# Boxes of a blocked triangular inverse requested ahead of weight tiles, with joins, sums and scaling at other places, in a hybrid decoder layer on one core

## Chip, core and metric

The kernel runs on one core of one Trainium2 chip. The metric is the device time of one execution in microseconds (us). The profile covers one execution; its span starts with the first instruction that the profile shows.

## What is computed

One decoder layer on 256 tokens of width 1024, in float32:

```python
proj = einsum('bsd,de->bse', rms_norm(h), w_in)
q, k, v = silu(causal_conv(proj[gdn part]))          # 8 heads of 128
a_mat = strict_lower(beta * k k^T * decay) + eye     # per head and chunk
u, w = triangular_solve(a_mat, [v * beta, k * beta * exp(g)])
o_a = gated delta rule with u, w over the chunks
y_a = (rms_norm(o_a) * silu(z)) @ w_branch_gdn
y_f = softmax(q_f k_f^T / 8 + forget terms) v_f @ w_branch_fox   # 16 heads of 64
h = h + (sigmoid(g_a) * y_a + sigmoid(g_f) * y_f) @ w_out
h = h + moe(rms_norm(h))       # 64 experts, top 8, plus a shared one
h = h + sigmoid(rms_norm(h) @ w_pg) * rms_norm(p @ w_ple)
```

The kernel takes chunks of 128 tokens, so there are 16 triangular problems of 128 x 128 (8 heads, 2 chunks).

## The kernel before

**Stages.** The convolved projections (12 products), then pairs of projection tiles, attention, the branch projections, and at the end the 32 pairs of experts, whose weights (6 MB a pair) stream through a ring of three slots.

**Pairs of tiles.** The weights of the projections come as tiles of 1024 x 512 (2 MB), numbered 0 to 23, into a ring of three buffers (`load(t)`, line 482). From tile 6 on two tiles make a pair: f0 (6, 7), f2 (8, 9), f4 (10, 11), z (12, 13), m0, m2, ya, yf, wo. A pair is multiplied in Strassen's manner: seven half products of four matmuls' worth of chunks (8 recorded matmuls, line 1084) instead of eight. They are numbered 1, 5, 2, 6, 3, 7, 4 (`product`, line 1087), need sums of token blocks, four sums of weight blocks (`weight_sum(p, k)`, lines 1861 to 1884) and are put together by `join(p, k)` (lines 1886 to 1906) on VectorE, with copies kept by ScalarE (`keep`, line 826). Parts 1 and 2 fill bank A, 5 and 3 bank C, 6 and 7 bank B, 4 bank D. Part 7 waits until join 6 of its pair is made (`u_made`). For f0, f2 and f4 the sums 1 and 3 are made by DMA: SyncE requests the first half block (`begin_sum`), GpSimd adds the second onto it (`add_first`, `add_third`). From z on VectorE makes them: `weight_sum(z, 1)` adds the left upper blocks of both tiles of the pair (line 1867) and so waits for tiles 12 and 13; part 5 of z waits for it.

**Banks.** The eight PSUM banks are handed out by a list written before the kernel (`bank_fills`, `placed`): each fill names its set of banks and takes the next of that set in turn. A fill waits until the fill before in its bank is drained. The half products of f0, f2 and f4 share FOX_BANKS = (7, 1, 2); the small products beside them (kk, bb, qk) take SIDE_BANKS = (4, 5, 6, 0, 3). By that list f4.A takes the bank of f2.C, which join 3 of f2 drains.

**The inverse.** The 16 problems are cut into diagonal blocks of 32 x 32, 64 in all. When VectorE has finished the blocks (bb.0 to bb.3, line 1930), SyncE writes the diagonal blocks to DRAM in four requests (`box_blocks`, line 506) and reads them back as 64 rows of 1024 words (line 508). VectorE inverts all 64 by a substitution of 31 steps of two operations (lines 1947 and 1949), behind some of which stand joins of f2 (JOINED) and sums of f4 (SUMMED). A copy (line 1954) makes the transposed inverse. `unbox_inverses` writes both to DRAM (line 513, two requests of 256 KB) and reads them back into the full matrices (line 518, eight requests of 64 KB). P5, X5, V5, P6 and V6 (lines 1247 and 1254) then build the inverse of 128 x 128 between the half products of z.

**Order of SyncE.** Its list is fixed, and a request that waits holds all behind it. Around the change it reads: tile 9, tile 10, box_blocks, a wait for qk.3, begin_sum(f4), tile 11, tile 12, tile 13, unbox_inverses, tile 14. Tile 11 waits for part 6 of f2, tile 12 for part 7 of f2, tile 13 for part 6 of f4 and the sum 4 of f4, tile 14 for part 7 of f4.

**Order of VectorE** behind the substitution: joins 6, 3, 7, 4 of f4, sums 1 and 3 of z, the scaling (two small and two large products, lines 1981 to 1988), fox_squares(0, 0) and (0, 1) (lines 1969 and 1970: squares of half a token block and their sums), the copy of cT, sum 2 of z, fox_squares(1, 0), sum 4 of z, fox_squares(1, 1).

Of the kernel before, what the change touches and what calls it, by code (L numbers as in the profile page):

```python
# [54 lines left out]
FOX_BANKS, SIDE_BANKS = (7, 1, 2), (4, 5, 6, 0, 3)  # L55
# [4 lines left out]
PAIRED = ("f0", "f2", "f4", "z", "m0", "m2", "ya", "yf", "wo")  # L60
F0_, F2_, F4_, Z_, M0_, M2_, YA_, YF_, WO_ = range(9)
# [6 lines left out]
OPENS = {1: "A", 5: "C", 6: "B", 4: "D"}  # L68
# [5 lines left out]
def bank_fills():  # L74

    f = ["ncols", "xT.0.0", "xT.0.1", "xT.1.0", "xT.1.1"]
    f += ["qkv.0", "cols", "smallT", "qkv.1", "small", "qkv.2", "cum", "qkv.3", "gbT"]
    for c in range(4, 8):
        f += [f"qkv.{c}", f"gb.{c - 4}", TQ_BESIDE[c]]
    for c in range(8, 12):  # L80
        f += [f"qkv.{c}", TQ_BESIDE[c]]
    f += ["tq.0.4", "tq.1.4"]
    g = [(name, ALL_BANKS) for name in f]
    for p, k, beside in FOX_ORDER:
        if k in OPENS:
            g += [(f"{PAIRED[p]}.{OPENS[k]}", FOX_BANKS)]
        g += [(b, SIDE_BANKS) for b in beside]
    g += [(name, ALL_BANKS) for name in ("cT", "z.A", "P5", "z.C", "X5", "V5", "P6.0", "P6.1", "z.B")]
    g += [("V6.0", (0,)), ("V6.1", (1,))]
    f = ["z.D"]  # L90
    for j in range(2):
        f += [f"tg.{j}", f"wT.{j}", f"u0.{j}"]
    for j in range(2):
        f += [f"o0.{j}", f"s1.{j}"]
    for j in range(2):
        f += [f"u1.{j}"]
    for j in range(2):
        f += [f"o1.{j}"]
    f += ["m0.A", "cb.0", "m0.C", "cb.1", "cb.2", "m0.B", "cb.3", "cb.4", "m0.D"]
    g += [(name, ALL_BANKS) for name in f]  # L100

    g += [(f"fT.0.{j}", HEAD_BANKS) for j in range(4)] + [("m2.A", PAIR_BANKS)]
    g += [(f"fT.1.{j}", HEAD_BANKS) for j in range(4)] + [(f"oT.{n}.{j}", HEAD_BANKS) for n in range(NT) for j in range(2)]
    g += [(name, HEAD_BANKS) for name in ("cb.5", "cb.6", "cb.7")] + [("m2.C", PAIR_BANKS)]
    g += [(f"s.{i}", HEAD_BANKS) for i in range(4)]
    for i in range(8):
        for p, k in BESIDE_ATTENTION[i]:
            if k in OPENS:
                g += [(f"{PAIRED[p]}.{OPENS[k]}", PAIR_BANKS)]
        g += [(f"pT.{2 * i}", HEAD_BANKS), (f"pT.{2 * i + 1}", HEAD_BANKS)]  # L110
        if i < 6:
            g += [(f"s.{2 * i + 4}", HEAD_BANKS), (f"s.{2 * i + 5}", HEAD_BANKS)]
        g += [(f"pv.{i}", HEAD_BANKS)]
    g += [(f"yf.{q}", PAIR_BANKS) for q in "ACBD"]
    g += [(f"pT2.{n}", HEAD_BANKS) for n in range(NT)]
    g += [(f"mT.{n}.{j}", HEAD_BANKS) for n, j in BLOCKS] + [("e.0.0", HEAD_BANKS)]
    g += [(f"wo.{q}", PAIR_BANKS) for q in "ACBD"]
    f = [f"hT.0.{j}" for j in range(2)] + ["e.0.1", "e.1.0"] + [f"hT.1.{j}" for j in range(2)]
    g += [(name, LAST_BANKS) for name in f]
    return g + [("e.1.1", (1,)), ("routerT", (0,)), ("router", (2,)), ("sg", (7,)), ("rank", (4,))]  # L120
# [14 lines left out]
def program(nc, x, p, norm_mix, w_in, conv_w, a_log, dt_bias, gdn_norm, fox_f_bias, q_norm, k_norm,  # L135
# [3 lines left out]
    with ctx:  # L139
# [227 lines left out]
        def ps(name):  # L367
            return bank[place[name][0]]

        def wait_filled(eng, name):  # L370
            b, turn = place[name]
            eng.wait_ge(filled[b], turn + 1)
# [14 lines left out]
        W_QKV, W_PAIRED = 0, 6  # L387
# [74 lines left out]
        def _(sp):  # L462
# [62 lines left out]
            for t in range(3, len(wtiles) - 1):  # L525
                if t == W_PAIRED:
                    begin_sum(F0_)
                if t == W_PAIRED + 3:
                    sp.wait_ge(qkss, 8)
                    begin_sum(F2_)  # L530
                if t == W_PAIRED + 5:
                    box_blocks()
                    wait_filled(sp, "qk.3")
                    begin_sum(F4_)
                if t == W_PAIRED + 2 * Z_ + 2:
                    unbox_inverses()
                load(t)

# [1164 lines left out]
        def _(dve):  # L1703
# [48 lines left out]
            for c2 in range(12):  # L1752
                nm = f"qkv.{c2}"
                wait_filled(dve, nm)
                for s in range(4):
                    for i in range(2):
# [4 lines left out]
                        if s == 0:  # L1761
                            k = step(v.tensor_scalar(dst, src, wcol, None, ALU.mult))
                        else:
# [4 lines left out]
                            else:  # L1768
                                k = step(ins)
# [90 lines left out]
            def weight_sum(p, k):  # L1860

                b00, b01, b10, b11 = halves_of(p)
                if k == 1:
                    for i in range(2):
                        tile = W_PAIRED + 2 * p + i
                        dve.wait_ge(w_loaded[tile % A_SLOTS], 16 * (tile // A_SLOTS + 1))
                    ins = v.tensor_tensor(wdif[p], b01, b00, ALU.add)
                if k == 3:
                    dve.wait_ge(t_made, sums_made(p, 1))
                    ins = v.tensor_tensor(b01, b11, b01, ALU.add)  # L1870
                if k == 2:
                    if p < Z_:
                        tile = W_PAIRED + 2 * p + 1
                        dve.wait_ge(w_loaded[tile % A_SLOTS], 16 * (tile // A_SLOTS + 1))
                        dve.wait_ge(sum1_made, 16 * (p + 1))
                    else:
                        dve.wait_ge(t_made, sums_made(p, 1))
                    dve.wait_ge(half_filled, 3 * p + 1)
                    ins = v.tensor_tensor(b00, b11, wdif[p], ALU.add)
                if k == 4:  # L1880
                    dve.wait_ge(t_made, sums_made(p, 2))
                    dve.wait_ge(half_filled, 3 * p + 2)
                    ins = v.tensor_tensor(wdif[p], b10, b00, ALU.add)
                ins.then_inc(t_made, 1)

            def join(p, k):

                name = PAIRED[p]
                d01, d11, d10 = (result(p, n, j) for n, j in BLOCKS[1:])
                if k == 6:  # L1890
                    dve.wait_ge(kept, 2 * p + 1)
                    dve.wait_ge(half_filled, 3 * p + 3)
                    v.tensor_tensor(d01, ps(f"{name}.B")[:, :], m1[p], ALU.subtract).then_inc(u_made, 1)  # L1893
                if k == 3:
                    wait_filled(dve, f"{name}.C")
                    dve.wait_ge(u_made, p + 1)
                    close(v.tensor_tensor(d01, d01, ps(f"{name}.C")[:, :], ALU.add), f"{name}.C")  # L1897
                if k == 7:
                    wait_filled(dve, f"{name}.B")
                    close(v.tensor_tensor(d10, m1[p], ps(f"{name}.B")[:, :], ALU.subtract), f"{name}.B")  # L1900
                    dve.wait_ge(kept, 2 * p + 2)
                    wait_drained(dve, f"{name}.B")
                    v.tensor_tensor(d11, m5[p], d10, ALU.subtract).then_inc(c11_made, 1)
                if k == 4:
                    wait_filled(dve, f"{name}.D")
                    close(v.tensor_tensor(d10, d10, ps(f"{name}.D")[:, :], ALU.add), f"{name}.D")
# [33 lines left out]
            dve.wait_ge(l_loaded, 16)  # L1940
            dve.wait_ge(zeroed, 1)
            lb, xb = (q.rearrange("p (i j) -> p i j", i=BLK) for q in (lblk, xblk))
            JOINED, SUMMED = {11: 6, 17: 3, 20: 7, 21: 4}, {22: 2, 25: 4}
            for k in range(BLK - 1):
                m = BLK - 1 - k
                outer = rank1[:, 0:m * (k + 1)].rearrange("p (i j) -> p i j", i=m)
# [7 lines left out]
            v.tensor_copy(vblk.rearrange("p (j i) -> p j i", j=BLK), xblk.rearrange("p (i j) -> p j i", i=BLK)).then_inc(solved, 1)  # L1954

            join(F4_, 6)
            join(F4_, 3)
            join(F4_, 7)
            join(F4_, 4)
            for p in (F0_, F2_):  # L1960
                for q in "ACBD":
                    wait_drained(dve, f"{PAIRED[p]}.{q}")
# [2 lines left out]
            def fox_squares(n, half):  # L1965

                src = fox[:, n, D * half:D * half + D]

                seq(v.tensor_tensor(at(TPB, 1024), src, src, ALU.mult))
                ins = v.tensor_reduce(f_ss[:, n, 16 * half:16 * half + 16], at(TPB, 1024).rearrange("p (a b) -> p a b", a=16), AX.X, ALU.add)  # L1970
                if half:
                    ins.then_inc(fss, 1)
                    dve.wait_ge(fss, n + 1)
                else:
                    seq(ins)

            weight_sum(Z_, 1)
            weight_sum(Z_, 3)
            dve.wait_ge(geg, 2)
            dve.wait_ge(tq_copied, 6)  # L1980
            seq(v.tensor_tensor(be_s, eg_s, gb[:, 16:32], ALU.mult))
# [4 lines left out]
            k1 = qk[:, 1, D:2 * D].rearrange("p (h d) -> p h d", h=GH)  # L1986
            v.tensor_tensor(q1, q1, bc(eg_s[:, 8:16], 2, P), ALU.mult).then_inc(scaled, 1)
            v.tensor_tensor(k0, k0, bc(et_s[:, 0:8], 2, P), ALU.mult).then_inc(scaled, 1)

            fox_squares(0, 0)  # L1990
            fox_squares(0, 1)
            wait_filled(dve, "cT")
            close(v.tensor_copy(rowsT[:, 1, :], ps("cT")[0:48, 0:P].bitcast(BF16)), "cT")
            weight_sum(Z_, 2)
# [92 lines left out]
            for g in range(8):  # L2087
                if g < 7:
                    maxima(g + 1)
                f = 2 * g  # L2090
# [98 lines left out]
            k = [step(onto(n, j, m1[WO_], ALU.subtract if j else ALU.add)) for n, j in BLOCKS[1:]]  # L2189
# [282 lines left out]
```

## Time and profile before

| | |
|---|---|
| median of 3 runs | 902.4 us (901.75 to 904.97) |
| the profiled execution | 902.0 us |
| its span | 900.3 us |
| TensorE busy (PE) | 882.2 us, 98% |
| VectorE busy (DVE) | 521.0 us, 58% |
| ScalarE busy (ACT) | 196.3 us, 22% |
| GpSimd busy (POOL) | 58.2 us, 6% |
| moved by DMA | 275.53 MB, mean 306 GB/s |
| first small products of f0's pair to the last of z's | 103 to 224 us of the span |
| expert stage | 414 to 867 us of the span |

Busy time is the time in which an engine runs an instruction. SP is SyncE, PEld TensorE's weight loads. A row of a timeline gives start, duration, engine, line, operation, output from inputs, shape, count, and in brackets the idle time of the engine before it and what ended that.

### The profile page before, as it was taken

The page shows a single profiled execution, that of the slowest core. Times are in us where ns is not written, and L with a number is a line of the kernel's source. Part 1 is how long each engine was busy: PE and PEld are TensorE (multiplying, and loading weights), DVE is VectorE, ACT ScalarE, POOL GpSimd, SP SyncE. Part 2 cuts the span into 40 slices and gives each one's busy share as a digit, 9 for nine tenths or more (in the row PEclk, how much of TensorE's full clock was granted, in tenths as well). Part 3 has the DMA queues.
Part 4 walks back from the last instruction along what each step waited for, and adds up shares of the span by engine and source line. Part 5 has one row for each costly group of instructions (what it writes and reads, how often), then busy time and mean ns, then how long its engine had stood idle before and what let it go on. Part 6 is the DMA issues. An engine that isn't in the chain of part 4 may idle for free.

```text
span 900.3 us, 21078 instructions
## 1 busy us (share of the span) xinstructions
PE 882.2 (98%) x9169; PEld 503.8 (56%) x9170; DVE 521.0 (58%) x975; ACT 196.3 (22%) x398; POOL 58.2 (6%) x78
## 2 busy tenths in 40 slices
PE   7999999899999999999999999999999999999997
PEld 6888754345745454456555555555555555555543
DVE  3656866967677886865434345343435444445367
ACT  2214200012426651242111111101011111111122
POOL 2011200106200000020000000000000000000010
PEclk9999999999999999999999999999999999999999
DMA  8653888774151438978999999999999999999951
GB/s 247 228 202 110 225 275 247 194 234 148 40 186 47 141 117 333 383 307 332 401 421 420 423 421 422 422 422 422 422 422 422 422 422 422 422 422 422 415 209 49
DMA packets 69188, 275.53 MB, mean 306 GB/s; under 512 B 11498, under 2 KB 14171, under 8 KB 44315
## 3 DMA queue, kind: packets, MB, share of 16 engines
q1 hardware_dynamic: 67114, 268.68, 75.6%
q0 software_dynamic: 2016, 6.29, 3.7%
q8 instruction: 27, 0.44, 0.2%
q14 instruction: 15, 0.11, 0.0%
q10 hardware_dynamic: 16, 0.00, 0.0%
HBM read 269.99 MB, written 1.84 MB: 302 GB/s over the span
## 4 chain that ended last, share of the span: by engine, by line
PE 87%; DVE 6%; DMA 3%; ACT 1%; SPq 1%; issue 1%; POOL 0%; DVEq 0%; POOLq 0%; ACTq 0%
PE bank L1554 25%; PE bank L1084 17%; PE bank L1535 13%; PE bank L1199 9%; PE bank L1505 5%; PE bank L1518 5%; PE bank L1663 2%; PE bank L1061 2%; PE bank L1574 1%; DMA lbox<-arena 1%; PE bank L1153 1%; DVE arena L1949 1%; DVE arena L1947 1%; PE bank L1463 1%; PE bank L1474 1%
## 5 line engine op out<-in xcount | busy, mean ns | idle before, releaser
L1554 PE MATMUL bank<-arena 128*32 128x256 f32 x4096 | 227.2, 379 | 0.3 <-DVE arena L2278 0.3
L1554 PEld LDWEIGHTS bank<-arena 128*32 128x32 f32 x4096 | 132.8, 110 | 100.5 <-issue 18.6
L1084 PE MATMUL bank<-arena 128*128 128x512 f32 x344 | 154.4, 597 | 1.6 <-DVE arena L1893 1.6
L1535 PE MATMUL bank<-arena 128*32 128x512 f32 x1024 | 116.5, 595 | 0.5 <-ACT arena L991 0.5
L1084 PEld LDWEIGHTS bank<-arena 128*128 128x128 f32 x344 | 63.6, 190 | 77.1 <-issue 76.6
L1199 PE MATMUL bank<-actT,arena 128*128 128x256 f32 x384 | 85.3, 380 | 0.4 <-DVE actT L1731 0.4
L1199 PEld LDWEIGHTS bank<-actT,arena 128*128 128x128 f32 x384 | 72.0, 190 | 10.4 <-issue 1.1
L989 ACT ACTIVATE arena<-bank 128x256 f32<-128x256 f32 x32 | 12.3, 384 | 267.9 <-PE bank L1554 267.9
L2329 DVE COPY arena<-bank 128x512 f32<-128x512 f32 x32 | 22.1, 692 | 81.9 <-PE bank L1535 81.9
L2314 DVE SCALAR_TENSOR_TENSOR arena<-arena,gslot,bank 128x256 f32<-128x256 f32 x32 | 15.4, 480 | 90.0 <-ACT arena L989 90.0
L1084 PE MATMUL bank<-arena,actT 128*128 128x512 f32 x144 | 65.2, 596 | 2.3 <-DVE arena L1897 2.3
L1535 PEld LDWEIGHTS bank<-arena 128*32 128x32 f32 x1024 | 30.0, 109 | 59.9 <-issue 57.5
L2319 DVE COPY arena<-bank 128x512 f32<-128x512 f32 x31 | 21.4, 692 | 67.9 <-PE bank L1505 67.9
L1505 PE MATMUL bank<-onehot,arena 128*128 128x64 bf16 x1536 | 50.0, 193 | 0.0
L1505 PEld LDWEIGHTS bank<-onehot,arena 128*128 128x128 bf16 x1536 | 49.0, 98 | 1.0 <-issue 0.7
L772 ACT ACTIVATE arena<-bank 128x512 f32<-128x512 f32 (+2 forms) x60 | 30.1, 524 | 79.9 <-PE bank L1061 40.5
L1084 PEld LDWEIGHTS bank<-arena,actT 128*128 128x128 f32 x144 | 26.5, 190 | 33.1 <-issue 33.0
L681 POOL TENSOR_SCALAR stat<-stat 128x1 f32<-128x1 f32 x6 | 1.6, 267 | 618.2 <-ACT arena L1027 468.3
L2345 DVE TENSOR_TENSOR arena<-arena,masks 128x1024 f32<-128x1024 f32 x31 | 38.0, 1225 | 1.1
L995 ACT ACTIVATE arena<-bank 128x512 f32<-128x512 f32 x32 | 19.1, 597 | 66.1 <-PE bank L1535 66.1
L1061 PE MATMUL bank<-ident,arena 128*128 128x128 f32 (+1 forms) x206 | 28.1, 275 | 5.4 <-DMA arena<-in_norm_mix 3.4
L1061 PEld LDWEIGHTS bank<-ident,arena 128*128 128x128 f32 (+1 forms) x206 | 23.6, 141 | 15.7 <-issue 10.4
(321 smaller groups left out, 998.1 us busy)
## 6 DMA issues: line engine op xcount, KB each, us to landing
arena<-in_we_gate SPq DMA_DIRECT2D x32, 2048.0 KB, 17.4
arena<-in_we_up SPq DMA_DIRECT2D x31, 2048.0 KB, 18.6
arena<-in_we_down SPq DMA_DIRECT2D x29, 2048.0 KB, 17.6
arena<-in_w_in SPq DMA_DIRECT2D x17, 2048.0 KB, 9.1
arena<-in_we_down SPq DMA_DIRECT2D x6, 1024.0 KB, 8.3
arena<-in_w_in SPq DMA_DIRECT2D x5, 1024.0 KB, 10.0
arena<-in_w_branch_gdn SPq DMA_DIRECT2D x2, 2048.0 KB, 8.1
arena<-in_w_branch_fox SPq DMA_DIRECT2D x2, 2048.0 KB, 8.3
```

The source lines that it names most:

```text
L772: a.activation(dst, ps(name)[:, 0:cols_used] if len(dst.shape) == 2 else ps(name)[:, 0:cols_used].rearrange("p (a b) -> p a b", a=dst.shap ...
L995: a.activation(y[:, 0:WT], bank[4][:, :], ACT.Copy).then_inc(y_ready[0], 1)
L1061: ins = t.transpose(o[0:w, i * P:i * P + rows_in], v, ident[0:rows_in, 0:rows_in])
L1084: ins = t.matmul(o[:, :], lhs[:, c, :], rhs[:, c, :], start=fresh and c == 0, stop=c == HC - 1, skip_group_check=not fresh)
L1199: ins = t.matmul(o[:, i * S:i * S + S], w[:, c, col:col + P], actT[:, c, :], start=(c == 0), stop=(c == KC - 1))
L1505: ins = t.matmul(bank[5 + half][:, c * P + n * 2 * CAP:c * P + (n + 1) * 2 * CAP], hparts[:, k, n, (4 * half + c) * P:(4 * half + c + 1) * P],
L1518: ins = t.matmul(bank[2 * n + j][:, :], spread[s][hp, :], yparts[j][k][hp, :], start=False, stop=False, skip_group_check=True)
L1535: ins = t.matmul(bank[4 + j][i * CAP:i * CAP + CAP, :], hidT[:, c, i * CAP:i * CAP + CAP], d_in[s][:, i % 2, c * D + WT * j:c * D + WT * j ...
L1554: ins = t.matmul(bank[4][i * CAP:i * CAP + CAP, m * DE:m * DE + DE], xg[:, c, i * CAP:i * CAP + CAP], gu_in[s][:, m, i % 2, c * DE:c * DE ...
L2319: v.tensor_copy(xg[:, 4:8, :], bank[6][:, :].rearrange("p (c s) -> p c s", c=4)).then_inc(xb_ready, 1)
L2329: v.tensor_copy(y[:, WT:D], bank[5][:, :]).then_inc(y_ready[1], 1)
L2345: v.tensor_tensor(y, y, yhigh, ALU.subtract).then_inc(y_rest, 1)
```

## The change

- The third pair (f4) takes its banks from SIDE_BANKS.
- SyncE makes the requests of box_blocks, with the wait for qk.3 and begin_sum(f4) behind them, ahead of tile 10 instead of ahead of tile 11.
- SyncE makes the requests of unbox_inverses ahead of tile 13 instead of ahead of tile 14.
- The joins of f2 stand behind steps 7, 15, 18 and 19 of the substitution instead of 11, 17, 20 and 21, the sums of f4 behind 21 and 23 instead of 22 and 25.
- Behind the substitution VectorE runs join 6 of f4, fox_squares(0, 0), join 3, the scaling, joins 7 and 4, fox_squares(0, 1), and only then the sums 1 and 3 of z.

```diff
@@ bank_fills
         if k in OPENS:
-            g += [(f"{PAIRED[p]}.{OPENS[k]}", FOX_BANKS)]
+            g += [(f"{PAIRED[p]}.{OPENS[k]}", FOX_BANKS if p < F4_ else SIDE_BANKS)]
@@ SyncE
-                if t == W_PAIRED + 5:
+                if t == W_PAIRED + 4:
                     box_blocks()
                     wait_filled(sp, "qk.3")
                     begin_sum(F4_)
-                if t == W_PAIRED + 2 * Z_ + 2:
+                if t == W_PAIRED + 2 * Z_ + 1:
                     unbox_inverses()
                 load(t)
@@ VectorE
-            JOINED, SUMMED = {11: 6, 17: 3, 20: 7, 21: 4}, {22: 2, 25: 4}
+            JOINED, SUMMED = {7: 6, 15: 3, 18: 7, 19: 4}, {21: 2, 23: 4}
...
             join(F4_, 6)
-            join(F4_, 3)
-            join(F4_, 7)
-            join(F4_, 4)
             for p in (F0_, F2_):
                 for q in "ACBD":
                     wait_drained(dve, f"{PAIRED[p]}.{q}")
...
-            weight_sum(Z_, 1)
-            weight_sum(Z_, 3)
+            fox_squares(0, 0)
+            join(F4_, 3)
             dve.wait_ge(geg, 2)
             dve.wait_ge(tq_copied, 6)
             seq(v.tensor_tensor(be_s, eg_s, gb[:, 16:32], ALU.mult))
...
             v.tensor_tensor(k0, k0, bc(et_s[:, 0:8], 2, P), ALU.mult).then_inc(scaled, 1)
-
-            fox_squares(0, 0)
+            join(F4_, 7)
+            join(F4_, 4)
             fox_squares(0, 1)
+            weight_sum(Z_, 1)
+            weight_sum(Z_, 3)
             wait_filled(dve, "cT")
```

## Rows read from the trace of the kernel before

**Rows 1.** The page's first part: busy time of each engine.

```profile
PE 882.2 (98%) x9169; PEld 503.8 (56%) x9170; DVE 521.0 (58%) x975; ACT 196.3 (22%) x398; POOL 58.2 (6%) x78
```

**Rows 2.** Waits of TensorE over the span: total us, times, longest.

```profile
PE bank L1084 <- DVE arena L1897: 2.3, 1, 2.3
PE bank L1084 <- DVE arena L1893: 1.6, 1, 1.6
PE bank L1247 <- DMA arena<-vbox: 1.5, 1, 1.5
```

**Rows 3.** Timeline of TensorE, 159 to 200 us.

```profile
159.21 3.67 PE L1084 MATMUL bank<-arena 128*128 128x512 f32 x8 [1.64 <-DVE arena L1893]
165.19 3.67 PE L1084 MATMUL bank<-arena,actT 128*128 128x512 f32 x8 [2.31 <-DVE arena L1897]
...
189.62 3.70 PE L1084 MATMUL bank<-arena,actT 128*128 128x512 f32 x8
194.80 1.20 PE L1247 MATMUL bank<-arena 32*32 32x32 f32 x64 [1.48 <-DMA arena<-vbox]
195.93 3.70 PE L1084 MATMUL bank<-arena 128*128 128x512 f32 x8
```

**Rows 4.** Timeline of VectorE, 125 to 194 us.

```profile
125.98 2.47 DVE L1930 TENSOR_TENSOR arena<-arena,bank 128x512 f32<-128x512 f32 x4
...
143.95 2.29 DVE L1883 TENSOR_TENSOR arena<-arena 128x2048 f32<-128x2048 f32 x1 [0.83 <-PE bank L1084]
150.06 0.18 DVE L1947 TENSOR_TENSOR arena<-arena 64x31 f32<-64x31 f32 x1 [3.82 <-DMA arena<-lbox]
...
155.03 0.37 DVE L1947 TENSOR_TENSOR arena<-arena 64x207 f32<-64x207 f32 x1
...
180.53 1.04 DVE L1954 COPY arena<-arena 64x1024 f32<-64x1024 f32 x1
...
191.50 2.29 DVE L1867 TENSOR_TENSOR arena<-arena 128x2048 f32<-128x2048 f32 x1
```

**Rows 5.** Timeline of SyncE's requests, 130 to 194 us, merged over their waits.

```profile
130.54 11.50 SPq L506 DMA_DIRECT2D lbox<-arena  x4
...
150.74 28.82 SPq L482 DMA_DIRECT2D arena<-in_w_in  x3
...
188.85 1.93 SPq L518 DMA_DIRECT2D arena<-xbox  x4
...
192.95 0.49 SPq L482 DMA_DIRECT2D arena<-in_w_in  x1
```

**Rows 6.** The chain that ended last, 182 to 189 us.

```profile
182.12 6.67 DMA vbox<-arena
```

**Rows 7.** DMA request at 816.8 (KB, us to landing); timeline of TensorE.

```profile
arena<-in_we_gate SPq DMA_DIRECT2D x1, 2048.0 KB, 31.2
854.22 7.09 PE L1554 MATMUL bank<-arena 128*32 128x256 f32 x128
```

**Rows 8.** GpSimd at 134; DMA landings: block, stores, tile 14, all tiles.

```profile
134.43 0.87 POOL L709 DMA_DIRECT2D arena<-arena  x1 [14.18 <-DMA arena<-in_w_in]
...
arena<-lbox SPq DMA_DIRECT2D x1, 256.0 KB, 3.8
out<-arena SPq DMA_DIRECT2D x3, 256.0 KB, 2.0
arena<-in_w_in SPq DMA_DIRECT2D x1, 2048.0 KB, 9.2
DMA to landing us min/median/max: 7.7/8.7/13.8
```

**Rows 9.** Granted clock in the tail (third last figure); timeline of TensorE.

```profile
898.50:899.00 0.50, 0.00 (x0) 0.00 (x0) 0.00 (x0) 0.00 (x0) 0.00 (x0) 0.66 0.74 250
...
3.54 1.75 PE L1129 MATMUL bank<-ident 128*128 128x128 f32 x7
271.27 3.66 PE L1061 MATMUL bank<-ident,arena 128*128 128x128 f32 x32
```

## Prediction, made before the kernel was changed

> **What bounds the kernel now.** The page comes first: TensorE is busy 98% of the span, and VectorE's 521 us count only where TensorE waits for it [rows 1]. The question is where TensorE idles near the change. Its waits answer it [rows 2]: 2.3 us until the third-part join of the second pair (line 1897) had drained a bank, 1.6 us until the first join of that pair (line 1893), 1.5 us until the inverses were back in SBUF. That is 5.4 us in all. The timeline of TensorE [rows 3] places them: I write (pair, part) for a half product; (f2, 7) starts at 159.21, 1.64 us late; (f4, 1) at 165.19, 2.31 late; (z, 1) at 189.62, P5 at 194.80, 1.48 late, and (z, 5) at 195.93.
>
> The first two waits are VectorE's doing. It starts the substitution at 150.06, when the boxed blocks have landed, having finished its last sum at 146.2 [rows 4]; the first join stands behind step 11, the second behind step 17. The third wait is the way back: the inverse is finished at 181.57, the boxes are in DRAM 6.67 us after the second request, and eight requests take SyncE from 188.85 to 192.95 [rows 5, 6]; the last lands 2.3 us after it was made.
>
> Behind the mixers nothing adds to a gain or a loss or takes from it. The last pair's gate tile lands 31.2 us after its request at 816.8, at 848.0, while TensorE opens that pair at 854.22 [rows 7]. The requests follow TensorE's progress, and 6.2 us would be left even if they didn't.
>
> **The way out (boxes ahead of tile 10).** SyncE makes the four box requests once bb.3 is drained, at 128.45 (125.98 + 2.47 [rows 4]); before, the first went out at 130.54 [rows 5], behind the 2 MB of tile 10. Now the boxes follow tile 9, which landed at 134.4 (its landing releases GpSimd's transfer [rows 8]). After tile 10's landing, 10.4 us after 130.0, the last box took 5.8 us more, to 146.2; 134.4 + 5.8 gives 140.2, and the block needs the 3.8 us of before [rows 8]: 144.0. GpSimd's accumulating transfer of 1 MB runs beside this in both kernels. Bounds: 138.2 (134.4 + 3.8) and 150.06 (no gain). I take 144.0. VectorE isn't free until 146.2, so the substitution starts there, 3.86 us earlier; 2.2 us of delay would be hidden. What it is moved past: begin_sum(f4) goes from 146.84 to about 141, behind qk.3; GpSimd's add on it starts sooner and its next add still waits for tile 11, with the clearing of xi and vi behind it as before; tile 10 goes from 130.0 to about 141.5 and lands near 151 for a use at 161; tile 11 stays at 150.74, set by (f2, 6) [rows 5]. All of this costs nothing.
>
> **Joins, sums and banks.** Step 8 began at 155.03 [rows 4], 4.97 us after the start, so the first join is now at 151.17, after (f2, 6), which ends at 150.74. (f2, 7) starts when (f2, 3) ends, and the 1.64 us go. (f4, 1) takes bank 4, last used by bb.3, in place of bank 2 of f2.C, so the 2.31 us go too; f4.C, f4.B and f4.D take banks 5, 6 and 0, emptied long before. Followed down with the old step times, the second join is at 158.7 ((f2, 3) ends at 157.6), the third at 162.0 ((f2, 7) ends at 161.2), the first sum at 166.5 ((f4, 1) ends at 164.7), the second at 170.3 ((f4, 5) ends at 168.2). None waits and no operation is added, so the inverse is done at 181.57 - 3.86 = 177.7. TensorE is 1.64 + 2.31 = 3.95 us ahead: (z, 1) starts at 185.67 and ends at 189.36.
>
> **The way back (ahead of tile 13).** This is the costly part. The requests come at 177.74 and 178.26. Before, they stood behind tile 13, requested at 179.2, just before the end of the third request in SyncE's row, 150.74 + 28.82 [rows 5]. Alone they are bounded by the 2.0 us of an output store of this size and the 3.8 us of the block's load [rows 8]; I take 3.0, near the middle, since there are two: 181.3. The eight requests take 4.1 us as before; the last lands at 187.2, under (z, 1), and the 1.48 us go. P5 runs from 189.36 to 190.5.
>
> But tile 13 is requested behind the eight, at 185.4 instead of 179.2. The tile directly behind them before, tile 14, landed 9.2 us after its request at 192.95; all 2 MB loads of this stretch took between 7.7 and 13.8 [rows 8]. I take 9.2, the same place in the queue: 194.6. weight_sum(z, 1) adds half of tile 12 to half of tile 13, so VectorE, done with the joins and the scaling at about 190.1, stands before it until 194.6, and 2.29 us later [rows 4], at 196.9, (z, 5) may start. Queued behind this wait on VectorE are weight_sum(z, 3), the copy of cT and weight_sum(z, 2); they end by 201.7 and are needed at 210. TensorE pauses from 190.5 to 196.95, 6.45 us, and is then 1.0 us later than before.
>
> The Trainium skill (DMA: Bandwidth & Descriptors, Anatomy of one DMA) fits a transfer as about 2.0 us fixed plus its bytes at 436 GB/s; an estimate by it gives 3.2 us for the two boxes and 6.8 us for tile 13, and the sum would be 2.2 us lower. No 2 MB load of this stretch was that quick, so the rows decide.
>
> **The clock.** TensorE's last matmul ends at 895.3; its granted clock averages 0.66 from 898.5 to 899.0 [rows 9] and is 0.50, 1.2 GHz, behind that: it fell about 3.3 us into that idle time. The new pause is longer, so I expect (z, 5) to restart at 1.2 GHz. The price: the first transposes of the kernel, after an idle start, come 250 ns apart (7 in 1.75 us) and those at 271.27 come 114 ns apart (32 in 3.66 us) [rows 9]; 16 slow ones ran to 7.2, and the next, at 7.87, were at the later rate. So at least 3.67 us ran at half rate, which loses 1.8, and at most 4.3 us, which loses 2.2. I take 2.0; bounds 0 (the clock stays) and 3.7 (twice that stretch). The Trainium skill (TensorE: Matmul & The Clock Gate, HAM oscillation) says that waits for DMA between bursts of matmuls make the next burst start at half clock; by that rule the 2.0 us are paid, without it the sum is 2.0 lower.
>
> **Moved work on VectorE.** fox_squares(0, 0) fills 178.3 to 180.8, ahead of (f4, 3), done at 182.1; the scaling fills 182.7 to 185.4, ahead of (f4, 7), done at 185.6. Without this cover they would cost their 2.5 and 2.7 us; here the wait for tile 13 covers them too. f4.C's bank is drained at 182.7 for z.A at 185.7, f4.B's at 186.3 for P5.
>
> **Sum.** -3.95 - 1.48 + 6.45 + 2.0 = +3.0. The profiled execution took 902.0 us (span 900.3), so 905.0; the median of the three runs is 0.4 above it, so 905.4.
>
> **Rivals.** A, the forecast, 0.57: +1.7 to +5.5 with the bounds of the landings and the clock, 904 to 908.
>
> B, 0.17: the pause is cheap, because tile 13 lands in 7.7 us or the clock stays: +3.0 - 1.5 or +3.0 - 2.0, with both -0.5: 902 to 904. For it: 7.7 us was seen. Against: 9.2 in the like place, and the tail's clock. The fit of the Trainium skill (DMA: Bandwidth & Descriptors) quoted above would put the time here.
>
> C, slower, 0.14: the way out isn't sped up, so the change doesn't do what it says. The boxes' 128-byte pieces and GpSimd's accumulating transfer hold each other up, the block lands at 150.06 as before, and inverse and tile 13 come 3.86 us later: +3.0 + 3.9 = +6.9, 909.3. It decides from a landing after 146.2. Against it: 2.2 us of slack.
>
> D, faster, 0.12: tile 13 lands in time and all three waits go: -5.4, 897.0. For it: TensorE's path has nothing else in its way. Against: tile 13 must land by 188.2, 2.8 us after its request.
>
> **How the numbers follow.** A measurement of this kernel can tell about 0.5%, 4.5 us, from no change. Slower by more: C and a quarter of A, 0.28. Faster by more: most of D, 0.10. Within: 0.62. The range runs from a little below B, 899, to 909; it leaves out most of D and half of C, about 0.2.
>
> **What would show it.** Line 1947 starts at 146.2; TensorE's waits for lines 1893 and 1897 are gone; (z, 1) starts near 185.7; P5 doesn't wait; then line 1084 waits some 6.4 us for line 1867, with the clock at 0.5 for some microseconds. Tile 13 lands near 194.6. The forecast is wrong if that wait is under 2 us (D), if line 1947 starts after 148 (C), or if a new wait stands behind 215.

## The result and the profile after

The changed kernel takes 905.22 us (median of 19 runs, 904.07 to 907.15), the kernel before 903.35 (19 runs, 901.29 to 905.98): ratio 1.0022, 95% interval 1.0014 to 1.0031, so 1.3 to 2.8 us slower. That is inside the range and within 0.5%; the forecast was 905.4. The median of before over 19 runs is 1 us above that of the three runs that the prediction had, so the difference was forecast as 3.0 and came out as 1.9.

The page's first part for the changed kernel, beside [rows 1]: TensorE's share is the same, VectorE's work too.

```profile
PE 885.7 (98%) x9170; PEld 506.1 (56%) x9170; DVE 521.0 (58%) x975; ACT 196.2 (22%) x398; POOL 54.0 (6%) x78
```

The waits of TensorE (total us, times, longest) of the changed kernel, the answer to [rows 2]:

```profile
PE bank L1084 <- issue: 7.8, 1, 7.8
PE bank L1061 <- DMA arena<-in_norm_mix: 2.3, 1, 2.3
PE bank L1061 <- DVE arena L1726: 2.0, 2, 1.6
PE bank L1061 <- DVE arena L1906: 0.5, 1, 0.5
```

The three waits of before, 5.4 us in all, are gone, and one of 7.8 us stands in their place. One more difference lies ahead of all that was changed: by tile 9's request this execution is already 1.02 us later than the first one of before (122.96 against 121.94). The waits of line 1061 at the start don't explain it (4.8 us in all here, 5.0 there); the granted clock does in part: it is 0.50 from 10 to 12 us here and averages 0.85 and 0.80 in the 2 us before and after, where the first profile of before shows 1.00, and the slowest matmul of line 1199 below 20 us takes 765 ns against 483. Below, "counted from tile 9" means less that start. The timeline of TensorE, the answer to [rows 3]:

```profile
155.00 7.03 PE L1084 MATMUL bank<-arena 128*128 128x512 f32 x16
161.87 3.60 PE L1084 MATMUL bank<-arena,actT 128*128 128x512 f32 x8
...
186.21 3.70 PE L1084 MATMUL bank<-arena,actT 128*128 128x512 f32 x8
189.84 1.20 PE L1247 MATMUL bank<-arena 32*32 32x32 f32 x64
198.84 6.21 PE L1084 MATMUL bank<-arena 128*128 128x512 f32 x8 [7.80 <-issue]
204.98 2.12 PE L1247 MATMUL bank<-arena 32*32 32x32 f32 x128
```

(f2, 3) and (f2, 7) are now one row without a gap, (f4, 1) follows at 161.87, and P5 follows (z, 1) at once. Then comes the pause, and (z, 5) takes 6.21 us instead of 3.70. What it waited for, "issue" here, is seen on VectorE, the answer to [rows 4]:

```profile
147.18 0.17 DVE L1947 TENSOR_TENSOR arena<-arena 64x31 f32<-64x31 f32 x1
...
177.63 1.06 DVE L1954 COPY arena<-arena 64x1024 f32<-64x1024 f32 x1
...
189.35 1.22 DVE L1967 TENSOR_REDUCE f_ss<-arena 128x16 f32<-128x1024 f32 x1
196.45 2.29 DVE L1867 TENSOR_TENSOR arena<-arena 128x2048 f32<-128x2048 f32 x1 [5.88 <-DMA arena<-in_w_in]
```

The substitution starts at 147.18, 146.16 less the later start, and isn't held by its load. VectorE then stands 5.88 us before sum 1 of z, line 1867, until tile 13 has landed; (z, 5) starts when that sum ends, at 198.8. SyncE's requests, the answer to [rows 5]:

```profile
129.57 3.26 SPq L506 DMA_DIRECT2D lbox<-arena  x4
136.88 0.54 SPq L508 DMA_DIRECT2D arena<-lbox  x1
...
178.71 0.47 SPq L513 DMA_DIRECT2D xbox<-arena  x1
...
182.86 1.93 SPq L518 DMA_DIRECT2D arena<-xbox  x4
184.84 2.08 SPq L518 DMA_DIRECT2D arena<-vbox  x4
187.02 38.82 SPq L482 DMA_DIRECT2D arena<-in_w_in  x4
```

The last row begins with tile 13, requested at 187.02. Its landing is VectorE's start at 196.45, so 9.4 us. The landings of the boxes (KB each, us to landing), from requests at 129.6 to 132.0, at 136.9 and at 179, the answer to [rows 6, 8]:

```profile
lbox<-arena SPq DMA_DIRECT2D x4, 64.0 KB, 4.8
...
arena<-lbox SPq DMA_DIRECT2D x1, 256.0 KB, 8.3
...
xbox<-arena SPq DMA_DIRECT2D x1, 256.0 KB, 2.9
vbox<-arena SPq DMA_DIRECT2D x1, 256.0 KB, 3.6
```

And the stretches around the pause (granted clock third from the end, then DMA share and GB/s), which [rows 9] answer to:

```profile
190.00:192.00 2.00, 1.04 (x64) 0.93 (x60) 0.57 (x1) 1.45 (x3) 1.25 (x2) 1.00 1.05 395
192.00:194.00 2.00, 0.00 (x0) 0.00 (x0) 0.00 (x0) 0.28 (x1) 2.00 (x1) 0.93 1.05 406
194.00:195.00 1.00, 0.00 (x0) 0.00 (x0) 0.00 (x0) 0.00 (x0) 1.00 (x1) 0.50 1.05 385
...
203.00:204.00 1.00, 1.00 (x2) 0.34 (x1) 1.00 (x2) 0.00 (x0) 0.00 (x0) 0.52 0.00 0
204.00:205.00 1.00, 1.00 (x5) 0.21 (x3) 0.96 (x2) 0.00 (x0) 0.00 (x0) 1.00 0.00 0
```

The clock is at 0.50, 1.2 GHz, from just before 194 until just before 204: some five microseconds of pause and 5.1 us of work.

### The profile page after: what moved, and what is told of

It reads as the page before. It is cut to its first block, busy times and chain, and to the rows that moved or that the text cites. A ratio compares the mean times of both kernels' runs of the same rounds, so it can differ in the third digit from the quotient of the medians.

```text
span 905.4 us, 21078 instructions
## 1 busy us (share of the span) xinstructions
PE 885.7 (98%) x9170; PEld 506.1 (56%) x9170; DVE 521.0 (58%) x975; ACT 196.2 (22%) x398; POOL 54.0 (6%) x78
## 4 chain that ended last, share of the span: by engine, by line
PE 94%; DVE 3%; issue 1%; ACT 1%; DMA 1%; POOL 0%; SPq 0%; DVEq 0%; POOLq 0%; ACTq 0%
PE bank L1554 25%; PE bank L1084 23%; PE bank L1535 13%; PE bank L1199 9%; PE bank L1505 5%; PE bank L1518 5%; PE bank L1663 2%; PE bank L1061 2%; PE bank L1153 2%; PE bank L1574 1%; PE bank L1463 1%; PE bank L1474 1%; PE bank L1293 1%; PE bank L1391 1%; ACT arena L772 1%
## 5 line engine op out<-in xcount | busy, mean ns | idle before, releaser
L1084 PE MATMUL bank<-arena 128*128 128x512 f32 x344 | 156.7, 605 | 7.8 <-issue 7.8
L995 ACT ACTIVATE arena<-bank 128x512 f32<-128x512 f32 x32 | 19.1, 597 | 66.1 <-PE bank L1535 66.1
L826 ACT ACTIVATE arena<-bank 128x512 f32<-128x512 f32 x18 | 10.7, 595 | 103.7 <-PE bank L1084 103.7
```

Of the source, the lines that this page charges most:

```text
L995: a.activation(y[:, 0:WT], bank[4][:, :], ACT.Copy).then_inc(y_ready[0], 1)
L1084: ins = t.matmul(o[:, :], lhs[:, c, :], rhs[:, c, :], start=fresh and c == 0, stop=c == HC - 1, skip_group_check=not fresh)
```

## The experiments

**Theory 1**: the change takes out the three waits as meant, and what it loses is tile 13's late request and the clock that falls in the pause. **Theory 2**, the rival in each run, puts the loss, or the worth of a part, elsewhere.

**1. The way back alone put back.** Edit, on the changed kernel:

```diff
-                if t == W_PAIRED + 2 * Z_ + 1:
+                if t == W_PAIRED + 2 * Z_ + 2:
                     unbox_inverses()
```

> The changed kernel with the way back put behind tile 13 again, everything else kept. Theory 1 (the loss is tile 13 requested too late, and the half clock that follows the pause): tile 13 is requested near 175 and lands near 183.5, so part 5 of z waits for nothing, P5 waits about 1 us for the inverses, the clock stays at 1.00, and the time is 4 to 5 us under the kernel before, about 898.5. Theory 2 (the loss sits elsewhere, in the earlier boxes, the banks or the new order on VectorE): it stays within 2 us of the changed kernel, 903 to 906.

Measured: 899.88 us (899.06 to 900.38) against 902.82, ratio 0.9965 (0.9951 to 0.9978): 3.2 us less than before. Its timeline of TensorE:

```profile
185.63 3.70 PE L1084 MATMUL bank<-arena,actT 128*128 128x512 f32 x8
191.14 1.37 PE L1247 MATMUL bank<-arena 32*32 32x32 f32 x64 [1.81 <-DMA arena<-vbox]
192.44 5.14 PE L1084 MATMUL bank<-arena 128*128 128x512 f32 x8
```

Tile 13 is requested near 175 again and (z, 5) follows P5 at once. Theory 2 is out: one line turns the loss into a gain. The gain is short of the 4 to 5 us expected, and the rows show two places: P5 waits 1.81 us, since the boxes stand behind tile 13 again, and (z, 5) takes 5.14 us. The clock fell here after a wait under 2 us, which the kernel before had had without a fall.

**2. The way back alone moved.** Edit, on the kernel before:

```diff
-                if t == W_PAIRED + 2 * Z_ + 2:
+                if t == W_PAIRED + 2 * Z_ + 1:
                     unbox_inverses()
```

> The kernel before with the way back alone moved ahead of tile 13. Theory 1: tile 13 lands near 198.5 of the span, part 5 of z starts near 201 instead of 195.9 and at half clock for its length, so 7 to 8 us over the kernel before, about 910. Theory 2: within 1.5 us of the kernel before.

Measured: 908.43 us (907.62 to 908.65), ratio 1.0059 (1.0046 to 1.0072), 5.3 us more. Its timeline of TensorE:

```profile
165.78 5.37 PE L1084 MATMUL bank<-arena,actT 128*128 128x512 f32 x8 [2.31 <-DVE arena L1897]
...
195.53 1.20 PE L1247 MATMUL bank<-arena 32*32 32x32 f32 x64
201.29 5.08 PE L1084 MATMUL bank<-arena 128*128 128x512 f32 x8 [4.56 <-issue]
```

Alone the move costs what theory 1 says in kind, 2 us less in size: with a pause of 4.56 us the half product behind it pays 1.4 us, and the start of this execution was 1.14 us later, which puts (z, 5) at 200.2 counted as before was, against the 201 expected. The clock also fell behind the wait of 2.31 us ahead of (f4, 1), the same wait that in the first profile of before left it at 1.00; the 1.7 us lost there came off the later pause, since (z, 5) starts when tile 13 and its sum allow it.

**3. Filling the pause in part.** Edit, on the changed kernel:

```diff
+            b, turn = place["z.C"]
+            pe.wait_ge(drained[b], turn)
+            for _ in range(40):
+                t.transpose(bank[b][:, 0:P], ident[:, :], ident[:, :])
             product(Z_, 5)
```

> The changed kernel with 40 transposes of the identity into the bank that part 5 of z opens next, in the pause behind P5 (4.6 us of the 7.8; their output is overwritten and the result is the same). Theory 1: tile 13 comes as late as before, but the clock stays at 1.00 and part 5 of z takes 3.7 instead of 6.2 us, so 2.5 us under the changed kernel. Theory 2 (the half clock has nothing to do with idle time): part 5 still takes 6.2 us, and the time doesn't move.

Measured: 905.45 us (903.52 to 906.64), ratio 1.0028 (1.0019 to 1.0037): nothing gained. TensorE:

```profile
189.72 4.58 PE L1263 MATMUL bank<-ident 128*128 128x128 f32 x40
197.66 5.37 PE L1084 MATMUL bank<-arena 128*128 128x512 f32 x8 [3.36 <-issue]
```

The expectation missed: 3.36 us of idle time were left, and the clock fell behind them. The clock is 1.00 up to 198 and averages 0.67 from 198 to 200, so it fell when (z, 5) had already begun; (z, 5) takes 5.37 us, between the 3.7 of theory 1 and the 6.2 of theory 2. The run doesn't separate the theories, and led to the next.

**4. Filling it whole.** As the run before, with 68 transposes.

> The changed kernel with 68 transposes of the identity in the pause behind P5, 7.8 us at 114 ns each, so that TensorE has no idle time there (40 left 3.4 us idle, and the clock fell all the same). Theory 1 (idle time lets the clock fall): the clock is 1.00 throughout, part 5 of z takes 3.7 us, and the time is about 2.5 us under the changed kernel, 902.5 to 903.5. Theory 2 (the clock isn't worth anything here, since the end is set by something else): no change against the changed kernel, 905.

Measured: 904.44 us (903.43 to 904.92), ratio 1.0011 (1.0002 to 1.002). TensorE:

```profile
191.02 7.65 PE L1263 MATMUL bank<-ident 128*128 128x128 f32 x68
198.84 3.67 PE L1084 MATMUL bank<-arena 128*128 128x512 f32 x8 [0.17 <-issue]
202.44 2.12 PE L1247 MATMUL bank<-arena 32*32 32x32 f32 x128
```

(z, 5) starts at the same 198.84 as in the changed kernel, takes 3.67 instead of 6.21 us, and the span is 902.9 against 905.4. Between the profiled executions the clock is worth 2.5 us, all of which reaches the end. Between the medians it is 0.8 (904.44 against 905.22; by the ratios 1.0, and the two intervals, 1.0002 to 1.0020 and 1.0014 to 1.0031, overlap). The expectation of 902.5 to 903.5 missed. I come back to this below.

**5. The way out put back.** Edit, on the changed kernel:

```diff
-                if t == W_PAIRED + 4:
+                if t == W_PAIRED + 5:
                     box_blocks()
```

> The changed kernel with the way out put back ahead of tile 11. Theory 1: the substitution starts at 150 as before, inverse and tile 13 come 3.9 us later than in the changed kernel, and the time is 3.5 to 4 us above it, about 909. Theory 2 (the earlier boxes bring nothing): as the changed kernel, 905.

Measured: 908.03 us (907.61 to 910.66), ratio 1.0055 (1.0042 to 1.0068), so about 3 us above the changed kernel where 3.5 to 4 were expected. TensorE, with its waits:

```profile
172.85 3.67 PE L1084 MATMUL bank<-arena 128*128 128x512 f32 x8 [1.47 <-issue]
...
191.63 1.20 PE L1247 MATMUL bank<-arena 32*32 32x32 f32 x64 [0.64 <-DMA arena<-vbox]
201.77 6.53 PE L1084 MATMUL bank<-arena 128*128 128x512 f32 x8 [8.94 <-issue]
```

Boxes requested early are worth what the forecast gave them: without that, (f4, 6) waits for its sum, the inverse and tile 13 come later ((z, 5) at 201.77, 3.9 us later counted from tile 9), and this is the price of rival C, 0.9 us short in the medians. Between the profiled executions, counted from tile 9, it is 4.5 us (786.9 against 782.4).

**6. The banks alone.** Edit, on the kernel before:

```diff
-            g += [(f"{PAIRED[p]}.{OPENS[k]}", FOX_BANKS)]
+            g += [(f"{PAIRED[p]}.{OPENS[k]}", FOX_BANKS if p < F4_ else SIDE_BANKS)]
```

> The kernel before with the new banks of the third pair alone. Theory 1 (up to P5 the end is set by the boxes, the substitution and the way back, not by TensorE): part 1 of f4 no longer waits 2.3 us, P5 waits 3.8 instead of 1.5 us for the inverses, and the time stays within 1.5 us of the kernel before. Theory 2 (a wait of TensorE is worth its length): 2.3 us less.

Measured: 901.81 us (900.13 to 903.9), ratio 0.9982 (0.9972 to 0.9992), 0.7 to 2.5 us less. TensorE:

```profile
159.52 5.37 PE L1084 MATMUL bank<-arena 128*128 128x512 f32 x8 [1.93 <-DVE arena L1893]
164.73 3.60 PE L1084 MATMUL bank<-arena,actT 128*128 128x512 f32 x8
...
194.42 1.20 PE L1247 MATMUL bank<-arena 32*32 32x32 f32 x64 [1.64 <-DMA arena<-vbox]
```

(f4, 1) doesn't wait, as expected. But P5 waits 1.64 and not 3.8 us, because (f2, 7) ran at half clock in this execution and used the time up; P5 itself starts 0.4 us earlier than in the kernel before. That is theory 1 in the profile. The median lies between the theories (1.6 us less), and the interval excludes only that nothing was won: the most that theory 1 allows (1.5 us) and the 2.3 us of theory 2 both lie in it. Every run has its mean granted clock on record, and on like clocks the gain is 1.6 us at 0.999 and above (six runs at a median of 901.05 against eight at 902.62) and 1.0 at 0.997 to 0.998 (902.43 against 903.41), nearer theory 1; it stays open.

**7. Half of the reads from ScalarE.** On kernel 1, the four requests that read vbox back are made by ScalarE ahead of `keep(Z_, 0)`:

```diff
+            act.wait_ge(zeroed, 3)
+            act.wait_ge(xv_boxed, 32)
+            for r in range(NB):
+                act.dma_start(vi[...], vbox[r].rearrange("b i j -> i b j")).then_inc(xv_loaded, 16)
```

> As the first one, with the four requests that read the transposed inverse back made by ScalarE, which is idle there, beside the other four on SyncE. Theory 1: the eight requests take 2.1 us instead of 4.1, P5 doesn't wait, and the time is 0.5 to 1.5 us under the first one, about 897.5. Theory 2 (the transfers, not the requests, take the time): no gain over the first one.

Measured: 900.17 us (897.9 to 901.54), ratio 0.9965 (0.9952 to 0.9978), no gain over kernel 1 in the median. TensorE:

```profile
191.74 1.20 PE L1251 MATMUL bank<-arena 32*32 32x32 f32 x64 [0.26 <-DMA arena<-vbox]
194.57 3.67 PE L1088 MATMUL bank<-arena 128*128 128x512 f32 x8 [1.62 <-issue]
```

The requests were the limit for P5: it waits 0.26 us and, counted from tile 9, starts 1.55 us earlier than in kernel 1 (tile 9's request is at 124.53 here, at 122.38 there). But (z, 5) then waits 1.62 us for sum 1 of z, which stands behind fox_squares(0, 1) on VectorE, so it starts when it did. One wait gave way to another, and the median didn't move. The eight runs fall into two groups by their mean granted clock: two at 0.999 took 897.90 and 898.15, six at 0.996 to 0.997 took 899.84 to 901.54, and kernel 1's five all lie at 0.996 to 0.997. The profiled execution is one of the six; its clock was at half for most of 9 to 16 us, long before the edit. So the median doesn't tell whether the edit is worth something when the clock holds.

**8. Part 5 ahead of P5.** From this: on kernel 1, sums 1 and 3 of z go ahead of fox_squares(0, 1), and part 5, which needs no inverse, covers the wait for it. ScalarE keeps part 5's copy ahead of P5's to match (not in the cut below).

```diff
             product(Z_, 1)
+            product(Z_, 5)
             pe.wait_ge(xv_loaded, 16 * 2 * NB)
             corner32("P5", ...
-            product(Z_, 5)
+            product(Z_, 2)
             wait_drained(pe, "P5")
...
-            product(Z_, 2)
+            product(Z_, 6)
             wait_drained(pe, "X5")
...
-            product(Z_, 6)
+            product(Z_, 3)
             wait_drained(pe, "V5")
...
-            fox_squares(0, 1)
             weight_sum(Z_, 1)
             weight_sum(Z_, 3)
+            fox_squares(0, 1)
```

> The changed kernel with the way back behind tile 13 again, sums 1 and 3 of z ahead of fox_squares(0, 1), and on TensorE part 5 of z ahead of P5, part 6 ahead of P6, part 3 ahead of V6. Theory 1: part 5 needs only its sum, made by 190, and covers the wait for the inverses; none of the waits at P5 is left, the clock stays, and the time is 2 to 3.5 us under the kernel with the way back alone moved, about 897. Theory 2 (the sums become the bound, part 5 waits for them and later steps of z for theirs): 899 to 901.

Measured: 897.06 us (896.58 to 897.61), ratio 0.993 (0.9917 to 0.9942), 6.3 us less than before, and the fastest. TensorE:

```profile
186.28 3.70 PE L1084 MATMUL bank<-arena,actT 128*128 128x512 f32 x8
190.55 3.67 PE L1084 MATMUL bank<-arena 128*128 128x512 f32 x8 [0.57 <-issue]
194.15 1.20 PE L1247 MATMUL bank<-arena 32*32 32x32 f32 x64
195.28 3.70 PE L1084 MATMUL bank<-arena,actT 128*128 128x512 f32 x8
```

0.57 us are left of all the waits, and no half product here runs at half clock. So rival D's time, 897.0, is there to be had. It took three moves: tile 13 ahead of the way back, the sums ahead of fox_squares(0, 1), and part 5 ahead of P5. The first alone gives 899.9 (kernel 1); what the other two give one by one, no run separates.

**9. More profiles of the same two kernels.** Kernels 1 and 6 had shown half products of 5.1 to 5.4 us behind waits of under 2 us, kernel 2 one behind 2.31 us. Theory 3, formed from that, was put to two more executions of the kernel before and one of the changed kernel.

> The kernel before, profiled once more. Theory 3 (formed after the kernels above: a wait of TensorE of 1.5 to 2.3 us lets its clock fall in some executions and not in others, as the half products behind such waits took 5.1 to 5.4 us in two of them): at least one of the half products behind the three waits takes 5 us or more instead of 3.7, or the median of before stands above its first profiled run for another reason. Rival: all three stay at 3.7, clock 1.00, and the spread of the times comes from the kernel's start alone (the first tile's request, 121.9 to 124.5 in the profiles so far).

> As the run ahead of it: the kernel before, a third profile. Theory 3: over the two, one half product or more at half clock. Rival: none.

> The changed kernel, profiled once more. Theory 3: the pause of 7.8 us recurs to within 0.3 us, since nothing in it depends on chance; the length of the stretch at half clock behind it differs, and part 5 of z takes between 5 and 7 us. Rival: pause and part 5 are as in the first profile, 7.8 and 6.2 us, and the start alone differs.

Measured: 902.83 and 902.96 us for the kernel before, 906.93 for the changed one. TensorE in the second profile of before:

```profile
159.35 3.67 PE L1084 MATMUL bank<-arena 128*128 128x512 f32 x8 [1.21 <-DVE arena L1893]
165.34 3.67 PE L1084 MATMUL bank<-arena,actT 128*128 128x512 f32 x8 [2.31 <-DVE arena L1897]
```

and in the third:

```profile
160.15 5.37 PE L1084 MATMUL bank<-arena 128*128 128x512 f32 x8 [2.05 <-DVE arena L1893]
166.13 3.67 PE L1084 MATMUL bank<-arena,actT 128*128 128x512 f32 x8 [0.61 <-DVE arena L1897]
```

For the kernel before theory 3 holds: the same wait lets the clock fall in one execution and not in another. In this profile it costs next to nothing (counted from tile 9 the spans are 778.4, 778.6 and 778.7), because the next wait shrinks by 1.7 us. In the second profile of the changed kernel the pause is 7.63 us and (z, 5) takes 6.20 us, 7.80 and 6.21 in the first, and the clock is back to 1.00 before 204 again. So there the rival of that expectation came true: theory 3 had the half clock's stretch differ between executions, and it didn't.

The timed runs say more on what the clock is worth. In the batch of 23 runs of before that kernels 4 to 6 and 8 were measured against, the eight with a mean granted clock of 0.999 and above have a median of 902.6, the six at 0.995 to 0.996 one of 904.8: 2.2 us. That is a correlation; where in those runs the clock fell isn't on record.

## Why the prediction came out as it did

The spans counted from tile 9: 778.4 before, 782.4 after (the second profiles: 778.6 and 782.4), so the profiled executions differ by about 4.0 us where 3.0 were forecast and the medians by 1.9. The range and the side were right, and the number is nearer than its steps deserve: in the profile the loss is larger than forecast, in the medians smaller. Step by step:

- **The way out.** Right in its end, wrong in its parts. The boxes landed 4.8 us after their requests, the last about 136.9, 135.9 counted as before was, not at 140.2; the block's load took 8.3 us, not 3.8. It ran beside GpSimd's accumulating transfer, requested at 135.7, while the 3.8 us had been read where that transfer was already in: requested at 134.43 it took 10.3 us, to 144.7, and the load was requested at 146.21. Together 144.2 against the forecast 144.0, 2 us before it was needed. The two terms cancelled by luck; the bound that held the step was VectorE's last sum, and the start at 146.16 is the forecast to 0.1 us.
- **Joins, sums and banks.** Right: none of the joins or sums of the substitution waits, and the inverse is done at 177.67 (forecast 177.7). (z, 1) starts at 185.19, not 185.67: a wait taken out gives back a little more than its idle time, since half products in an unbroken row come 3.43 us apart and one behind a wait takes 3.67.
- **The way back.** Right: the 1.48 us went. The boxes took 3.6 us, inside the bounds of 2.0 and 3.8, where 3.0 was taken, and tile 13 was requested 0.6 us later for it.
- **Tile 13.** Right in kind: 9.4 us to landing against 9.2. The fit of the Trainium skill (DMA: Bandwidth & Descriptors, Anatomy of one DMA) gave 6.8. That section states the fit for transfers requested by GpSimd, and these are SyncE's; for a tile behind eight requests in small pieces it is 2.6 us short, and for the 256 KB of xbox, requested on an idle queue, its 2.6 is near the 2.9 measured.
- **The pause.** 7.80 us against 6.45. The 1.35 us are the sum of those small terms: TensorE there 0.5 earlier, SyncE 0.6 later, tile 13 0.2 slower.
- **The clock.** It fell, as forecast, and (z, 5) took 2.5 us more, forecast 2.0: the work at half clock lasted 5.1 us, where the forecast took at most 4.3 from the kernel's start (read there from the pace of the transposes alone; the granted clock reads 1.00 over them). The rule of the Trainium skill (TensorE: Matmul & The Clock Gate, HAM oscillation) holds here: the pause was followed by work at 1.2 GHz, and kernel 4, without the pause, ran at 2.4 GHz. In the timed runs kernel 4 gains only 0.8 us. The clock fell there too: the mean granted clock of all 19 runs of the changed kernel is 0.992 to 0.995, that of kernel 4's eleven 0.997 to 1.000, and the 10.1 us at half clock in the profile lower such a mean by 0.0056. But both profiles of the changed kernel (907.15 and 906.93) lie above its other 18 runs (904.07 to 905.90), and kernel 5's, with a pause of 8.94 us, above its other four (910.66 against 907.61 to 909.44), while those of before (902.0, 902.83, 902.96) and of kernel 4 (904.61) lie within theirs. So the profiled execution loses more at this pause than the others. Whether their pause is shorter or their half clock cheaper, no run here shows. Kernel 4 can't tell: its 68 transposes fill 7.65 us whatever tile 13 does, so a shorter pause would shorten the changed kernel's time and not its own, and the 0.8 us would be too small a figure for the clock.
- **The rivals.** D failed on its condition: tile 13 landed at 195.4, counted as before was, and not by 188.2. Kernel 1 takes that obstacle away and gets 899.9; kernel 8, with part 5 and the sums moved too, gets 897.1. C's price was 3 us above the changed kernel instead of 3.9.

## What to carry to other kernels

When a small urgent transfer is moved ahead of a large one in a fixed queue, ask who needs the large one and when: here 1.5 us won at one consumer cost 7.8 us at the next. Look first for work that needs neither of the two and put it between, as part 5 ahead of P5 did. And before a wait is taken off the path, follow the next one behind it to its own source: the 1.55 us that ScalarE's requests won at P5 went to a sum that stood behind other work.

## What was not expected of the hardware

TensorE's clock fell behind waits as short as 1.8 to 2.1 us in three executions (half products of 5.14 and twice 5.37 us) and stayed at 1.00 behind waits of 2.31 and 1.87 us in others; behind the same wait of 2.31 us it fell in kernel 2 (5.37 us). The length of the wait alone doesn't decide it. In kernel 3 it fell after (z, 5) had begun. The block's load of 256 KB took 7.7 to 8.4 us in the seven profiled executions in which it was requested within 1.3 us of GpSimd's accumulating transfer of 1 MB, and 3.6 to 4.1 us in the six in which that transfer was in.

And the kernel's start alone moves tile 9's request between 121.7 and 124.5 us from one execution to the next, which is more than most of the effects studied here. It goes with how fast TensorE's matmuls run between 7.6 and 20 us. Three executions request tile 9 at 121.7 to 121.96; none of their sixteen transposes behind 7.6 us takes over 334 ns. Four request it at 122.0 to 122.5; some of their transposes take 473 to 477 ns, and the products of line 1199 that follow are as quick as in the first three (483 ns at most). In the six that request it at 122.8 or later these products too are slow at first, up to 765 ns, at a granted clock of 0.50. The granted clock of the profile can't show the first part: it reads 1.00 from the span's start, also over the first transposes, which take 421 ns. So spans are better compared from a common event behind the start, and the mean granted clock of each run is worth a look before medians are compared.
